# Later mixers with the compressed branch between the projection tiles, and new orders in recurrence and first attention

## The reference, cut to what matters

```
# first block
p = ada_norm(x) @ w_in                      # projections of both mixers
y_a = rwkv7_mix(...)                        # LoRA products, recurrence over tokens, 12 heads
y_b = dilated_attention_mix(pq, pk, pv)     # "first attention": 3 groups x 4 heads
x += gate * rms_norm((sig(ga)*y_a + sig(gb)*y_b) @ w_out);  x += gate * swiglu(...)
# second block, for l in 0, 1
x += 0.5 * gate * swiglu(...)
proj = h @ w_in[l]                          # 16 tiles of q and k, 2 chunks of values and gates
kcmp, vcmp = compress(rope(kc)), compress(vc)          # windows of 32 -> MLP with gelu (NSA)
o_cmp = softmax(q @ kcmp) @ vcmp            # compressed branch
o = gated sum of o_cmp, selected, window;  fox and moba attention
x += gate * (concat(o) @ w_out);  x += 0.5 * gate * swiglu(...)
```

## Time and profile before

| | |
|---|---|
| median of 3 runs | 1880.12 us (1879.37 to 1882.17) |
| profiled execution | 1880.62 us, its span 1878.8 us |
| mean granted clock of TensorE | 0.980 |
| busy share PE, DVE, ACT, POOL | 93%, 55%, 33%, 10% |
| first attention | 190.2 to 247.2 us |
| LoRA products, recurrence | 249.8 to 391 us |
| later mixers, first product to projection | 926.3 to 1076.4 us, 1498.7 to 1647.8 us |

### The profile page before, as it was taken

How to read it: one execution, slowest core, us unless ns; L and a number is a source line. 1 busy time by engine, 2 the same in 40 slices (tenths; PEclk the granted TensorE clock), 3 DMA queues, 4 the chain that set the end, 5 groups by cost and what they waited for, 6 DMA issues and landing times.

```text
span 1878.8 us, 31066 instructions
## 1 busy us (share of the span) xinstructions
PE 1749.4 (93%) x12812; PEld 1521.3 (81%) x12812; DVE 1040.3 (55%) x1758; ACT 616.3 (33%) x950; POOL 187.6 (10%) x273
## 2 busy tenths in 40 slices
PE   1999888889989998999999899999999999899998
PEld 1787777868679998999886569998999886659997
DVE  5456224442267777787512457877777612545454
ACT  2010222221153336333311643335433301544333
POOL 0122223410100000000010400000000010400000
PEclk9999899999999999999998999999999999999999
DMA  9765100004358782887244048884778344045441
GB/s 367 274 250 207 57 1 3 3 9 175 139 219 317 301 341 98 335 310 302 105 179 160 16 168 328 296 304 182 299 302 323 157 179 160 1 146 212 165 198 45
DMA packets 49204, 358.50 MB, mean 191 GB/s; under 512 B 5456, under 2 KB 6096, under 8 KB 29264
## 3 DMA queue, kind: packets, MB, share of 16 engines
q1 hardware_dynamic: 49104, 357.09, 49.7%
HBM read 356.02 MB, written 1.05 MB: 190 GB/s over the span
## 4 chain that ended last, share of the span: by engine, by line
PE 82%; DVE 6%; issue 4%; ACT 4%; DMA 2%; POOL 1%; SPq 0%; POOLq 0%; DVEq 0%; ACTq 0%
PE psum L853 13%; PE psum L804 10%; PE psum L806 10%; PE psum L805 10%; PE psum L817 5%; PE psum L818 5%; PE psum L819 5%; PE psum L882 4%; PE psum L871 3%; PE psum L774 2%; PE psum L729 2%; PE psum L1101 1%; DMA ring<-in_ada 1%; DMA ring<-in_in 1%; DVE arena L1743 1%
## 5 line engine op out<-in xcount | busy, mean ns | idle before, releaser
L804 PE MATMUL psum<-split 128*128 128x256 f32 x1600 | 453.1, 283 | 2.8 <-DVE split L1586 2.8
L806 PE MATMUL psum<-split 128*128 128x256 f32 x1600 | 452.8, 283 | 0.0
L805 PE MATMUL psum<-split 128*128 128x256 f32 x1600 | 452.8, 283 | 0.0
L804 PEld LDWEIGHTS psum<-split 128*128 128x128 f32 x1600 | 307.0, 192 | 5.6 <-DVE split L1586 3.8
L805 PEld LDWEIGHTS psum<-split 128*128 128x128 f32 x1600 | 307.0, 192 | 1.8
L806 PEld LDWEIGHTS psum<-split 128*128 128x128 f32 x1600 | 307.0, 192 | 0.0
L1586 DVE TENSOR_TENSOR split<-ring,split 128x2048 fp32r<-128x2048 f32 x110 | 251.8, 2289 | 82.0 <-ACT split L1268 77.8
L853 PE MATMUL psum<-hT,ring 128*128 128x256 f32 x1280 | 286.0, 383 | 8.4 <-ACT hT L1321 4.4
L1268 ACT ACTIVATE split<-ring 128x2048 fp32r<-128x2048 f32 x110 | 210.6, 1914 | 237.4 <-PE psum L806 173.0
L853 PEld LDWEIGHTS psum<-hT,ring 128*128 128x128 f32 x1280 | 245.4, 192 | 44.2 <-ACT hT L1321 5.1
L1606 DVE TENSOR_TENSOR split<-ring_down,split 128x2048 fp32r<-128x2048 f32 x55 | 126.0, 2291 | 117.0 <-ACT split L1276 117.0
(11 more groups left out here) (357 smaller groups left out, 2258.7 us busy)
## 6 DMA issues: line engine op xcount, KB each, us to landing
ring<-in_up SPq DMA_DIRECT2D x55, 2048.0 KB, 10.4
arena<-in_ada SPq DMA_DIRECT2D x176, 512.0 KB, 6.4
ring_down<-in_down SPq DMA_DIRECT2D x55, 1024.0 KB, 4.9
ring<-in_in SPq DMA_DIRECT2D x19, 2048.0 KB, 8.5
ring<-in_ada SPq DMA_DIRECT2D x4, 2048.0 KB, 9.7
ring<-in_gates SPq DMA_DIRECT2D x4, 2048.0 KB, 7.6
ring_down<-in_w_out SPq DMA_DIRECT2D x3, 2048.0 KB, 10.1
ring<-in_w_out SPq DMA_DIRECT2D x3, 2048.0 KB, 9.0
```

The lines of the kernel that those rows point to most:

```text
L804: mm(dst, up_hi[:, h, a], h_hi[:, kt_], start=(kt_ == 0 and j % 2 == 0), stop=False, skip_group_check=True)
L805: mm(dst, up_hi[:, h, a], h_lo[:, kt_], start=False, stop=False, skip_group_check=True)
L806: last = mm(dst, up_lo[:, h, a], h_hi[:, kt_], start=False, stop=(kt_ == KD - 1), skip_group_check=True)
```

## The change

On PE all calls of `keep_warm` go, and the function with them.

*First attention:* `qk(i + 2)` moves behind the transposes of head i.

*Recurrence:* within `unit`, `outputs` and the products of `tail` the same products are issued kind by kind across the four 64x64 quarters of the array, where before all kinds of one quarter followed each other. `inv_n` gets a second buffer (`inv_ns`, in `raw`), and POOL makes it two levels ahead; `first_y` and `next_n` are interleaved. `av(ps)` moves from between two passes into level 0, and the wait for `y0_ready` ahead of the levels goes, on PE and DVE. `outputs(ps, 1)` moves between the two state steps; ACT and DVE handle unit 3 earlier.

*Later mixers:* the chunks come in the order 0, 4, 5, 1, 2, 3 (`IN2_ORDER`), so values and gates follow the first four tiles. The first compression weight gets a place of its own (`cmp_side`), and both compression weights are loaded ahead of the chunks. The small products of the compressed branch stand between tiles 4 to 15, and ACT and DVE take the evictions in between. `rotate(15)` moves behind `qk(0)`. The banks of scores and outputs change (`S_BANK`, `O_BANK`). Compressed scores alternate between the halves `e`.

```
-MIX2_CHUNKS = 8
+MIX2_CHUNKS = 7
+IN2_ORDER = (0, 4, 5, 1, 2, 3)
...
-        S_BANK, T_BANK, O_BANK = ((4, 5), (6, 0)), (7, 2), (1, 3)
+        S_BANK, T_BANK, O_BANK = ((0, 1), (4, 5)), (7, 2), (3, 6)
... SP, mixer
+                for c, part in enumerate(IN2_ORDER):
+                    a, w = IN2_AT[part], 8 * IN2_WIDTHS[part]
+                    used = (cm_full, 48 + 16 * l + 4 * (part + 1)) if part < 4 else (tm_full, 4 + 4 * l + 2 * (part - 3))
+                    load(g + c, T["in2"][l, :, a:a + w], used)
+                    if c == 1:
                         sp.wait_ge(down_done, FC * (2 + 2 * l))
                         sp.dma_start(side, T["cmp1"][2 * l + 1]).then_inc(side_loaded, 16)
+                        sp.wait_ge(apart_used, 32 + 4 * ADA_PER_FFN * (2 * l + 2))
+                        sp.dma_start(cmp_side, T["cmp1"][2 * l]).then_inc(cmp_loaded, 16)
... PE, first attention
                 for i in range(4):
-                    if i < 2:
-                        qk(i + 2)
-                    keep_warm(20, 0)
                     pe.wait_ge(s1_prob, i + 1)
...
-                    keep_warm(8, 0)
+                    if i < 2:
+                        qk(i + 2)
                     pe.wait_ge(s1_tr, 3 * i + 3)
... PE, recurrence: unit
+                    for kind in range(3):
+                        for r in range(2):
+                            for e in range(2):
+                                hs, out = half(e), bank[4 + e][half(r)]
...
+                                if kind == 2:
+                                    last = mm(out[:, 4 * C:5 * C], kr[hs, h, 0, chunk_of], b, start=True, stop=True)
+                                else:
+                                    mm(out[:, 2 * C * kind:2 * C * (kind + 1)], (b, k)[kind], kr[hs, h, :, chunk_of], start=True, stop=True)
... levels and tail
-                    pe.wait_ge(y0_ready, 4 * (ps + 1))
...
                         if j == 0:
+                            av(ps)
                             wait(pe, pass_done, ps)
...
-                    outputs(ps, 1)
...
+                        if step == 0:
+                            outputs(ps, 1)
... POOL
+                def next_n(ps, j, lp):
+                    n, four = ps * len(LEVELS) + j, slice(4 * lp, 4 * lp + 4)
+                    wait(pool, w_full, 2 * n + lp - 3)
+                    tt(inv_ns[n % 2][:, four], scores_of[ps % 2][:, four, 0], K("levels_t", j * C, (j + 1) * C).unsqueeze(1).broadcast_to([P, 4, C]),
+                       ALU.mult).then_inc(nl_ready, 1)
... ACT, mixer
-                channel_major(T2, base, qbase)
+                channel_major(T2, base, qbase, range(0, 4))
...
                 f(gt, bank[2][:, 0:P], ACT.Gelu_apprx_tanh).then_inc(gelu_ready, 1)
+                channel_major(T2, base, qbase, range(4, 11))
                 act.wait_ge(cs_sub, l + 1)
                 f(csm, csm, ACT.Exp, scale=SCALE).then_inc(cs_exp, 1)
+                channel_major(T2, base, qbase, range(11, 14))
                 act.wait_ge(cst_full, l + 1)
```

More of the change, by code:

```diff
@@ L835, in ffn_split, with tile, rotate, channel_major @@
                 down(FC - 1)
[L837 to L845, removed]
+            def tile(table, base, j, w):
+                wait(pe, cm_evac, since(base, j - 1))
+                n = j % 4
+                for k in range(KD):
+                    last = mm(bank[4 + j % 2][:, 0:S], w[:, k * 512 + n * P:k * 512 + n * P + P], hT[:, k, :],
+                              start=(k == 0), stop=(k == KD - 1))
+                last.then_inc(cm_full, 1)
+            def rotate(table, base, rbase, j):
+                kind, q, r, _ = table[j]
+                if r is None:
+                    return
+                pe.wait_ge(cm_evac, base + j + 1)
+                wait(pe, rope_used, since(rbase, r - 1))
+                mm(bank[6 + r % 2][:, 0:S], K(kind), raw[:, q % 3, 1:S + 1], start=True, stop=True).then_inc(rope_full, 1)
+            def channel_major(g, table, base, rbase):
                 for j in range(len(table)):
                     if j % 4 == 0:
[L849 to L855 removed]
+                        w = chunk(g + j // 4)
+                    tile(table, base, j, w)
                     if j:
[L857 removed]
+                        rotate(table, base, rbase, j - 1)
                     if table is T1 and j == KK_SUMMED:
@@ L986, in levels @@
                                 for r in range(2):
[L987 removed]
+                                    last = mm(bank[lp][half(r), m * C:(m + 1) * C], inv_ns[(q // 2) % 2][half(r), 4 * lp + m], xy[half(r), 0, m], start=True, stop=True)
                             last.then_inc(w_full, 1)
@@ L1108, in mixer2, with tiles_of @@
                 wait_ht(n)
-                channel_major(g, T2, base, rbase)
+                def tiles_of(part, w, *js):
+                    for j in js:
+                        tile(T2, base, j, w)
+                        if j % 4:
+                            rotate(T2, base, rbase, j - 1)
+                w = chunk(g + IN2_ORDER.index(0))
+                tiles_of(0, w, 0, 1, 2, 3)
+                w = chunk(g + IN2_ORDER.index(4))
+                token_half(w, 512, 4, 0)
+                rotate(T2, base, rbase, 3)
+                token_half(w, 512, 5, 1)
                 pe.wait_ge(row_ready, n + 1)
@@ L2174, in rwkv @@
                     carried(0, lp)
-                for n in range(4):
-                    first_y(0, n)
-                next_n(0, 0)
+                first(0)
                 for ps in range(PAIRS // 2):
@@ L2195, in rwkv @@
                     if beside:
-                        for n in range(4):
-                            first_y(ps + 1, n)
-                        next_n(ps + 1, 0)
+                        first(ps + 1)
                 pool.wait_ge(gn_dev, 1)
```

200 lines of the change are left out of this document (104 added, 96 removed).

## The result

The changed kernel takes **1818.26 us** (median of 4 runs, 1814.27 to 1822.38) against 1879.76 beside it: a ratio of 0.967, 95% interval 0.964 to 0.9701, so 61.5 us less. Its four times go with the mean clock, 1814.3 and 1814.6 at 0.980 and 0.981, 1821.9 and 1822.4 at 0.977 and 0.976; the profiled execution is the slowest of them (1822.38, span 1820.5), so a single execution of this kernel is good to about 4 us.

What follows compares the result with a forecast made beforehand. PE, through which 82% of the span passes, was taken to bound the kernel. Terms of 18 + 5 + 3 + 9 + 22 = 57 us off the profiled 1880.6, with the median 0.5 lower, gave 1824 us, range 1808 to 1862.

Steps and rivals of the forecast that it cites:

- the likeliest case: Whole kernel: the forecast of 1824 us itself, with 1812 to 1836 as its own range, chance 0.62.
- First attention: 18: First attention: removing 4 x 28 dummies (26 us of PE time) gains 18 us, between 15 and 26.
- The two bounds: First attention: values end at 220.6 by the POOL chain (gain 26 us) or 232 with a slow clock (gain 15).
- LoRA: 5: LoRA products: removing four times 8 dummies of 1.95 us saves 7.8, or 3.8 if all six pairs stay slow; taken as 5.
- First units: 3: First recurrence units: without dummies the loop takes 3.3 us against about 4.2, so three intervals give 3 us.
- Recurrence: 9: Recurrence: moved waits, pass borders and order by kind, minus 2 for half clock, together 9 us, between -2 and 17.
- The order by kind: Recurrence: same products issued kind by kind across quarters; at most half a unit's 1.5 us of scores, 3 us in the sum.
- `av` 3: Recurrence: 3 us for the two borders of passes, where `av` no longer stands alone.
- 5.0 us wait for POOL: Recurrence: of PE's 12.3 us idle, 5.0 wait for POOL; a second `inv_n` lets POOL run two levels ahead, worth 5.
- Later mixers: 22: Both later mixers: dummies go and waits lie beside tiles; 12.2 saved less 1.0, so 11 us each.
- The slow clock through the recurrence: Rival, recurrence: without dummies it may enter at half clock and stay; 1844 to 1878, about 1860 us; chance 0.17.
- The mixer wait: Rival, later mixers: one late link on ACT or DVE stops a tile on both layers, 14 us, 1838; chance 0.10.

## Why the prediction was right

1824 us were forecast, 1818.3 came, inside the range and in the likeliest case. (1880.1 less 57 is 1823.1; the forecast rounds it up.) The sum of 57 us stands against 58.3 between the spans, but the terms are less good than their sum: in the recurrence a term that was much too small and two that were not there cancelled, which was luck.

**What bounds the kernel** was read rightly: the dummies were most of the first attention's busy PE, and taking them out alone brought 16.8 us there.

**First attention: 18, measured 21.6.** Dummies 16.8, the order 4.4 to 4.8. The two bounds, the ends of the values at 220.6 and at 232, enclosed the real end (224.3), and I took a point too near the slow one. The last turn is 5.8 us by the chain named there.

**LoRA: 5, measured 3.4.** A little below the bound of 3.8 for six slow steps, and five of the six were slow in full, at 2.31 us each. With dummies in the wait ahead they take 1.27, and the stretch is 8.7 us shorter than before. The bound was itself a little high: a pair with its dummies took 3.05 us before and 1.27 takes it without, so eight dummies cost 1.78 and not 1.95.

**First units: 3, measured 0.** The step "without them the loop is scores, masking and hand-overs" priced the loop alone, at the full clock. Taking the dummies out saved 1.2 us here, at a mean clock of 0.90, and cost 1.2 in the first pass, at 0.96: in units and passes together nothing was left.

**Recurrence: 9, and with the units 12; measured 10.9.** Right in size by luck and wrong in its parts. The order by kind was mis-sized: 3 in the sum, and 11 measured by undoing it. I had priced only the units' scores, at most half of each where it was 0.81 of 1.37 us, and given outputs and state products nothing, although they stand on PE's path in every pass. The Trainium skill (TensorE: Matmul & The Clock Gate, "Part 3: Packing small matmuls") says that products in different groups of the array run concurrently. By it the prediction had 6 us more than my 3, and 9 is nearer to the 11. The trace agrees with it: rows start every 14 ns where it was 32. The second `inv_n` was to be worth 5, and `av` 3; undone one at a time, neither moved the second pass by more than 0.3 us. The step that failed is "5.0 us wait for POOL" as the price of a second `inv_n`: the view names the releaser that came last. With POOL early the wait ends by something else, and moving DVE's updates shows that the next link takes over there too. A chain from W over ACT's copy, P and DVE's update back to W would do this; that it is this chain was argued and not shown.

**Later mixers: 22, measured 24.6.** The mechanism and the size held. The fill waits at the start of attention remained, as the prediction said, and the half clock behind them cost about 2 us per mixer, which dummies recovered.

**Not in the sum:** the group norm and the gates, 3.5 us longer in one trace of the changed kernel and 0.1 in the other. The first products of the group norm (x6) in the first and in the second:

```profile
356.06 5.31 PE L1087 MATMUL psum<-arena,const 128*128 128x512 f32 x6 [0.69 <-ACT arena L1479]
```

```profile
357.92 2.84 PE L1087 MATMUL psum<-arena,const 128*128 128x512 f32 x6 [0.70 <-ACT arena L1479]
```

The same wait stands ahead of both; the clock fell in one execution and not in the other. The stretches differ by 3.4 us. That this makes part of the spread of 8 us between executions was not shown.

**The slow clock through the recurrence** had 0.17. Its place was right and its length wrong: the units ran at 0.62 and 0.50 in the two traces, the first pass at 0.95 and 0.91, the second at 1.00. PE recovered the full clock on its own small products. The Trainium skill (TensorE: Matmul & The Clock Gate, "Why this matters for your kernels") warns of gaps in which PE idles between bursts of products. The trace agrees: the clock is 0.54 in LoRA behind a wait of 2.62 us for ACT, and 0.50 from 990 us in the mixer behind waits of 1.51 and 2.52. **The mixer wait** (0.10) did not come: no tile waits in the 89.9 us.

## What to carry to other kernels

A dummy product that keeps the clock pays inside a wait and costs outside: 112 in the first attention cost 16.8 us, while 74, most of them placed where PE waited, gained 8. Small products that use one quarter of the array should go round all four quarters with one kind before the next kind. And before a wait is bought off with a buffer, look for the chain that ends just behind the named releaser; here a second buffer only renamed part of the wait, and moving DVE's updates only moved it.

## What the runs showed of the hardware

With four 64x64 quarters in turn, rows of fp32 products start every 14 ns (16 in 0.23 us), against 32 ns when several kinds follow each other within a quarter (48 in 1.53 us) and 31 ns when one kind goes round two quarters (16 in 0.46 us). The full clock returned while PE did only products of 64x64, at the start of the first pass (granted clock 0.50 from 262.1 to 265.5, with PE busy throughout, and 1.00 from 265.5 to 280), so small products can bring it back. The same kernel can enter a stretch at half clock in one execution and at the full clock in another, with the same wait ahead of it (0.69 and 0.70 us ahead of the group norm, whose six rows then took 5.31 and 2.84 us).
